# Attention output written as query rows with the values as moving operand, and a mix product from split rows and split output weights

## The reference

```python
h = modulate(rmsnorm(x, g_norm1), sh1, sc1)          # sh1, sc1, gt1, ... from the conditioning vector
p, pc = h @ w_in, hc @ w_in                          # [Fourier 256 | q 768 | k 768 | v 768]
f_out = fourier_mix(p[..., :256], w_fmix)            # (1024, 256)
# 12 heads of 64; a query sees an 8 x 16 window of keys (masked scores) and all 256 context keys, one softmax
na_out = neighbourhood_attention(q, k, v, kc, vc, rpb)   # (1024, 768)
y = concat([rmsnorm(f_out, g_out[:256]), rmsnorm(na_out, g_out[256:])], -1) @ w_out
x = x + gt1 * y
h2 = modulate(rmsnorm(x, g_norm2), sh2, sc2)
x = x + gt2 * hierarchical_moe(h2, ...)              # 32 experts, top 1 group of 4, top 2 of 8 experts
return rmsnorm(x, g_final)
```

## Time and profile before

| | us |
|---|---|
| median of 3 runs | 1379.69 |
| lowest and highest | 1378.57, 1381.49 |
| the profiled execution, its own time | 1377.49 |
| its span, first to last instruction | 1375.2 |
| attention, 371.9 to 571.1 | 199.2 |
| mix, to the end of the last route but one, 571.1 to 709.7 | 138.6 |

### The profile page before, as it was taken

One profiled execution on the slowest core, in us unless ns is written; L12 is line 12 of the kernel. 1 busy time (PEld: TensorE's weight loads), 2 busy tenths in 40 slices (PEclk: granted clock), 3 DMA queues, 4 the chain that ended last, 5 costly groups with the idle time before them and its releaser, 6 DMA issues. The chain is left out here.

```text
span 1375.2 us, 18282 instructions
## 1 busy us (share of the span) xinstructions
PE 1282.1 (93%) x7138; PEld 1020.7 (74%) x7138; DVE 919.9 (67%) x1084; ACT 706.8 (51%) x822; POOL 242.5 (18%) x184
## 2 busy tenths in 40 slices
PE   4799999998899999999976999999999999999965
PEld 1799888887688888645544788888888888888842
DVE  2556543330077877544356988999988988889848
ACT  3742121121266666411113877877778777787713
POOL 0000000001000010100001154254254263521000
PEclk8899999999999999999986999999999999999988
DMA  9548744442486553312124899999999999999755
GB/s 382 198 169 306 248 135 158 157 130 96 169 321 233 190 189 94 130 60 95 61 92 162 347 389 391 389 378 374 389 382 387 384 372 395 383 383 383 255 198 219
DMA packets 96568, 349.73 MB, mean 254 GB/s; under 512 B 14219, under 2 KB 48483, under 8 KB 68835
## 3 DMA queue, kind: packets, MB, share of 16 engines
q1 hardware_dynamic: 79731, 317.35, 61.6%
q10 hardware_dynamic: 7536, 14.42, 3.5%
q0 software_dynamic: 9216, 16.80, 3.2%
HBM read 319.68 MB, written 39.32 MB: 261 GB/s over the span
## 5 line engine op out<-in xcount | busy, mean ns | idle before, releaser
L1825 DVE TENSOR_TENSOR w_low<-raw,w_high 128x2048 fp32r<-128x2048 f32 x128 | 293.4, 2314 | 31.2 <-ACT w_high L1765 28.3
L1765 ACT ACTIVATE w_high<-raw 128x2048 fp32r<-128x2048 f32 x128 | 241.1, 1910 | 9.3 <-PEq L1141 9.3
L1825 DVE TENSOR_TENSOR w_low<-arena,w_high 128x2048 fp32r<-128x2048 f32 x64 | 146.4, 2289 | 30.0 <-ACT w_high L1765 30.0
L1765 ACT ACTIVATE w_high<-arena 128x2048 fp32r<-128x2048 f32 x64 | 122.2, 1909 | 5.2 <-DMA arena<-in_w_down 5.2
L1682 PE MATMUL p_g<-w_high,x_high 128*128 128x512 f32 x256 | 103.9, 406 | 3.2 <-DVE x_low L1830 3.2
L1724 POOL DMA_INDIRECT y_rows<-arena,row x32 | 49.3, 1540 | 325.4 <-ACT arena L1786 323.9
L1682 PE MATMUL p_u<-w_high,x_high 128*128 128x512 f32 x256 | 102.3, 400 | 0.0
L1682 PE MATMUL p_y<-w_high,h_high 128*128 128x512 f32 x256 | 99.7, 389 | 2.5 <-DVE h_low L1835 2.5
L1682 PE MATMUL p_a<-tokens_high,half_high 128*128 128x512 f32 (+1 forms) x272 | 101.8, 374 | 0.0
L1684 PE MATMUL p_g<-w_high,x_low 128*128 128x512 f32 x256 | 101.2, 395 | 0.0
L1683 PE MATMUL p_g<-w_low,x_high 128*128 128x512 f32 x256 | 101.0, 394 | 0.0
(11 more groups left out here) (286 smaller groups left out, 2751.6 us busy)
## 6 DMA issues: line engine op xcount, KB each, us to landing
raw<-in_w_gate SPq DMA_DIRECT2D x64, 1024.0 KB, 8.2
raw<-in_w_up SPq DMA_DIRECT2D x64, 1024.0 KB, 7.6
arena<-in_w_down SPq DMA_DIRECT2D x64, 1024.0 KB, 7.9
raw<-in_w_ada SPq DMA_DIRECT2D x24, 1024.0 KB, 7.0
low_home<-in_bias SPq DMA_DIRECT2D x92, 192.0 KB, 3.8
x<-qk_rows SPq DMA_DIRECT2D x6, 1664.0 KB, 8.0
raw<-in_w_chunks SPq DMA_DIRECT2D x9, 1024.0 KB, 5.4
qk_rows<-x SPq DMA_DIRECT2D x18, 512.0 KB, 2.7
```

Source lines behind the costliest of these rows:

```text
L1765: act.activation(x.high[i % SPLITS][:], x.raw[j][:, :], ACT.Copy).then_inc(high_ok, 1)
L1825: dve.tensor_tensor(x.low[i % SPLITS][:], x.raw[j][:, :], x.high[i % SPLITS][:], ALU.subtract).then_inc(low_ok, 1)
```

## The change

**Attention.** In `weigh` the operands change places: a block of turned probabilities, 128 keys by 128 queries, is stationary, and the 64 channels of the values move. The output tile has the queries on the partitions and is written into `s.x1`, columns hp*128 on. The reciprocal of the row sum is then a number per partition, so the transposed spread copy goes (11 transposes a step become 10, the DVE copy 896 columns become 768, and the copy at line 993 goes), and `normalise` multiplies by it directly. `gain` and the POOL additions go; the last eight steps square the finished row tiles on ACT. Five of the eight blocks of output weights are split into high and low on ACT and DVE in steps 16, 22, 28, 34 and 40. The gain is multiplied into the weights there. The first head pair is loaded into gaps of `s.x1` by four DMAs, the others into the arena.

**Mix.** Token tiles of the attention output and of the Fourier part are transposed (`turn_n`, 8 transposes a tile), split by `high` (ACT) and `low` (DVE), and multiplied with the split weights by `products`. The gate, scale and shift rows are written to DRAM by three DMAs in the attention stage and loaded back as broadcast rows, which replaces `spread`; `turn_f` and the sums over `s.acc` go. The last three blocks of weights are split at the start of this stage.

```diff
-                    for k in range(KEYS // P):
-                        for h in range(2):
+                    for h in range(2):
+                        for k in range(KEYS // P):
...
-                            last = pe.matmul(p_o[n % 2][h * HD:(h + 1) * HD, 0:P], v, probt[b][:, first:first + P],
+                            last = pe.matmul(p_o[n % 2][:, h * HD:(h + 1) * HD], probt[b][:, first:first + P], v,
...
-                    pe.wait_ge(inverted, n + 1)
-                    pe.transpose(p_t[:, 2 * KEYS:2 * KEYS + P], spread[b], s.ident[:]).then_inc(turned, 1)
...
+                    dve.tensor_tensor(rows(s.x1[:, i, hp * P:(hp + 1) * P]), rows(p_o[n % 2][:, 0:P]),
+                                      rinv[:, n % 4, :].unsqueeze(2).to_broadcast([P, 2, HD]), ALU.mult).then_inc(normed, 1)
...
+                for j, x in enumerate((s.gate1, s.scale2, s.shift2)):
+                    sp.dma_start(a.vec_rows[j].rearrange("(k p) -> p k", p=P), x[:], allow_slow_non_contiguous=True).then_inc(s.wo_in, 16)
...
+                    if n == NT:
+                        for k, dst in zip(MIX_ORDER, s.wo_raw):
+                            sp.dma_start(dst, a.w_out[k * P:(k + 1) * P, :].rearrange("p (b n) -> p b n", b=4)).then_inc(s.wo_in, 16)
...
+                def high(n, b):
+                    act.wait_ge(turned, 2 * run_n(n) + b + 1)
+                    if n >= 2:
+                        act.wait_ge(mixed, n - 1)
+                    act.activation(nt_high[n % 2][:, 4 * b:4 * b + 4, :], p_t[b][:].rearrange("p (k q) -> p k q", k=4), ACT.Copy).then_inc(split_high, 1)
...
+                high(0, 0)
                 act.wait_ge(pool_ok, 4)
-                act.wait_ge(sums_ok, 2)
                 act.activation(root[:, 0:2, :], ss[:, 0:2, :], ACT.Sqrt, bias=epsb[:, 0:1]).then_inc(rooted, 1)
...
+                for i in range(EARLY, KD):
+                    split(i)
+                high(0, 1)
...
+                low(0, 0)
                 norm_groups()
...
+                scale_f(0)
+                for i in range(EARLY, KD):
+                    split(i)
+                low(0, 1)
+                for n in range(1, NT):
+                    scale_f(n)
+                low(1, 0)
+                low(1, 1)
+                for n in range(NT):
                     residual(n)
-                    if n < NT - 1:
+                    move_x(n)
+                    if n + 2 < NT:
                         norm_x(n)
-                move_x(NT - 1)
-                norm_x(NT - 1)
+                        low(n + 2, 0)
+                        low(n + 2, 1)
+                    else:
+                        norm_x(n)
...
+                        last = products(pe, p_y[n % 2][:, h, :], nt_high[n % 2][:, i, :], nt_low[n % 2][:, i, :],
+                                        s.wo_high[i][:, w], s.wo_low[i][:, w], start=(i == 0), stop=(i == KD - 1))
...
+                turn_n(0, 0)
                 for n in range(NT):
...
+                    for h in range(2):
+                        mix(n, 0, h)
+                    if n == 0:
+                        turn_n(0, 1)
+                    else:
+                        turn_x(n - 1)
+                    mix(n, 1, 0)
+                    if n + 1 < NT:
+                        turn_n(n + 1, 0)
+                        turn_n(n + 1, 1)
+                    mix(n, 1, 1)
+                    if n == 0:
+                        route_shift()
+                    else:
+                        route(n - 1)
```

More of the change, by code:

```diff
@@ L605, in _ @@
                     act.activation(ft[:, i // 2, (i % 2) * 512:(i % 2 + 1) * 512], p_a[m % 3][:], ACT.Copy).then_inc(moved, 1)
-                act.wait_ge(roped[1], HP)
+                for w in range(2):
+                    act.wait_ge(roped[w], HP)
                 for u in range(AB, G + NT):
@@ L954, in _ @@
                                            accum_out=rsum[n % 2][:, h:h + 1]).then_inc(exped, 1)
-                    if n >= 6 and (n - 2) % 4 == 0:
-                        u = (n - 2) // 4 - 1
-                        gain(u // 2, u % 2)
-                gain(HP - 1, 1)
+                    if n in SPLIT_AT:
+                        split(SPLIT_AT[n])
+                    if n >= STEPS - NT + 3:
+                        square(n - (STEPS - NT + 3))
+                square(NT - 1)
             @block.vector
@@ L1011, in _ @@
                         normalise(n - 2)
+                    if n - 1 in SPLIT_AT:
+                        split(SPLIT_AT[n - 1])
             @block.tensor
@@ L1031, in far @@
                         first = P + LOC + h * L
-                        return pe.matmul(p_s[:, first:first + L], qp[b][rows, q], kc[b][rows, :], start=True, stop=True)
+                        return pe.matmul(p_s[:, first:first + L], h_.q[0][rows, i, :], h_.context[rows, :], start=True, stop=True)
                     far(0).then_inc(scored, 1)
@@ L1265, in norm_groups, with scale_f, low, split @@
                     step(tt(ratio[:], ratio[:], rstd[:, 0, :], ALU.mult))
[L1266 to L1275 removed]
+                def scale_f(n):
+                    ts(s.fout[:, n, :], s.fout[:, n, :], ratio[:, n:n + 1], None, ALU.mult).then_inc(scaled, 1)
+                def low(n, b):
+                    dve.wait_ge(split_high, 2 * n + b + 1)
+                    part = slice(4 * b, 4 * b + 4)
+                    tt(nt_low[n % 2][:, part, :], p_t[b][:].rearrange("p (k q) -> p k q", k=4), nt_high[n % 2][:, part, :], ALU.subtract).then_inc(split_low, 1)
+                def split(i):
+                    k = MIX_ORDER[i]
+                    dve.wait_ge(s.half_high, WO_FIRST + i + 1)
+                    quarters = lambda x: x[:].rearrange("p (b n) -> p b n", b=4)
+                    stt(quarters(s.wo_low[i]), s.wo_raw[i], s.vcol[:, 80 + k:81 + k], quarters(s.wo_high[i]), ALU.mult, ALU.subtract).then_inc(s.half_low, 1)
                 def residual(n):
@@ new lines, in mix @@
+                def mix(n, b, h):
+                    if b == 0 and h == 0 and n >= 2:
+                        pe.wait_ge(added, 2 * (n - 2) + 1)
+                    if h == 0:
+                        pe.wait_ge(split_low, 2 * n + b + 1)
+                    for i in range(4 * b, 4 * b + 4):
+                        if n == 0 and h == 0:
+                            pe.wait_ge(s.half_low, WO_FIRST + i + 1)
+                        w = slice(h * 512, (h + 1) * 512)
+                        last = products(pe, p_y[n % 2][:, h, :], nt_high[n % 2][:, i, :], nt_low[n % 2][:, i, :],
+                                        s.wo_high[i][:, w], s.wo_low[i][:, w], start=(i == 0), stop=(i == KD - 1))
+                    if b == 1 and h == 1:
+                        last.then_inc(mixed, 1)
@@ L1455, in route_shift @@
                     last.then_inc(logits, 1)
+                turn_n(0, 0)
                 for n in range(NT):
-                    last = pe.matmul(p_r[:, n:n + 1], s.acc[:, n * P:(n + 1) * P], s.ones[:, 0:1], start=True, stop=True)
-                last.then_inc(sums_ok, 1)
-                spread(0, s.gate1)
-                pe.wait_ge(s.wo_in, 16)
-                mix_na(0)
-                turn_f(0)
-                mix_na(1)
-                mix_f(0)
-                spread(2, s.scale2)
-                mix_f(1)
-                spread(3, s.shift2)
-                mix_na(2)
-                turn_f(1)
-                mix_f(2)
-                turn_x(0)
-                mix_na(3)
-                route_shift()
-                route(0)
-                turn_x(1)
-                mix_f(3)
-                route(1)
-                turn_x(2)
-                for n in range(4, NT):
-                    mix_na(n)
-                    if n == 4:
-                        route(2)
-                    turn_x(n - 1)
-                    mix_f(n)
-                    route(n - 1)
+                    for h in range(2):
+                        mix(n, 0, h)
+                    if n == 0:
+                        turn_n(0, 1)
+                    else:
+                        turn_x(n - 1)
[4 more added lines that the diff above has]
+                    mix(n, 1, 1)
+                    if n == 0:
+                        route_shift()
+                    else:
+                        route(n - 1)
                 turn_x(NT - 1)
@@ L2185, in build @@
         s.raw = [m.sb(f"raw{r}", [P, CHUNK]) for r in range(RING)]
-        flat = s.x1[:].rearrange("p a b -> p (a b)")
-        s.heads = [flat[:, (1 - b) * 4 * D:(1 - b) * 4 * D + 3 * N + L] for b in range(2)]
         s.vh = s.raw[2][:].rearrange("p (g n) -> p g n", g=16)
```

312 lines of the change are left out of this document (137 added, 175 removed).

## The result

The kernel after the change takes 1405.22 us in the median of four executions (1404.08 to 1406.08), the kernel before 1380.51 (1378.57 to 1381.49). The ratio is 1.018 with a 95% interval of 1.0163 to 1.0198: slower by 24.7 us. The forecast was 1406. The profiled execution of after took 1405.07 us with a span of 1403.2; for before these are 1377.49 and 1375.2.

What follows compares the result with a forecast made beforehand. The prediction took PE to bound attention and mix, the only stages touched. The profiled 1377.5 us + 39.4 for attention - 12.9 for the mix gave 1404.0, or 1406 us on the scale of the runs, with bounds of 1397 to 1421.

Steps and rivals of the forecast that it cites:

- What bounds the kernel: Attention and mix: PE bounds both, busy 193.5 of 199.2 us and 138.2 of 138.6 us.
- The attention step, +39.4: Attention: 20 full-array instructions at 0.108 us in `weigh` make a step 4.79 us against 3.97, +39.4 us in 48 steps.
- DMAs at nothing in attention: Attention: output weight loads, three scattered stores and first head pair's loads cost nothing; 5 us late would show once.
- The mix, -12.9: Mix up to the end of `route(6)`: 12.9 us gained, the 0.9 of the earlier stage start included; bounds -20 and -4.
- The 6.5 us of idle PE: Mix, first tile: PE stands still about 6.5 us, for late group norms and three weight splits ahead of `low(0,1)`.
- the second fall of the clock: Mix, behind the idle stretch of the first tile: PE's clock falls once more, costing 2.5 us.
- The first fall: Mix, first 24 split products: the clock falls to 1.2 GHz, costing 2.1 us.
- the tile: Mix, each steady token tile: split products, two transpose groups and `route` take 14.35 us against 16.39.
- 1 (loads do not count): Attention, `weigh`: second instruction or load does not count at 64 moving columns, 10 us gained there, total 1357; 6%.
- 2 (loads and movement add): Attention, `weigh`: load and movement times add, 20 x 0.053 us more each step, +51 us, total 1457; 4%.
- 3 (the mix gains nothing): Mix: the ACT, DVE, PE chain or late norms take what the products give, total 1419; 10%.
- 4 (the start costs nothing): Mix start: no cost there, for instance if router weights land earlier, total 1399; 8%.

Runs made afterwards that it cites:

- e1: The changed kernel with each value matmul moving 128 columns of values in place of 64; attention stage 241.4 us, 1406.5 us in one run.
- e2: The changed kernel with 64 queries stationary in place of 128, the others left out; attention stage 202.9 us, total time not comparable.
- e8: e5 with the three scattered row stores issued twice in the old place; 1368.6 us, 0.9937 of the kernel before.
- e3: The changed kernel with the norms' root on ACT no longer waiting for the scaled router weights; 1400.7 us, 1.0157 of the kernel before.
- e4: The changed kernel with the old attention (values stationary, heads side by side) and the new mix kept; 1371.2 us, 0.9944 of the kernel before.
- e5: e4 with the norms' root no longer waiting for the scaled router weights, the edit of e3; 1359.2 us, 0.9858 of the kernel before.
- e7: e5 with the three scattered row stores issued behind the attention stage's last load; 1356.9 us, 0.9843 of the kernel before.
- e6: The changed kernel with two broadcast gate row loads issued behind the router weights' load, not ahead; 1402.0 us, 1.0167 of the kernel before.

## Why the prediction was right, step by step

**What bounds the kernel.** PE bounds both stages after the change too, but for the first tile of the mix, and the sum could be made of PE's distances and the one wait there.

**The attention step, +39.4.** Measured 4.81 us for 4.79: `score` 1.38 as said, `turn` 1.15 as said, `weigh` 2.28 for 2.26. An instruction with 128 by 128 loaded and 64 columns moving costs 0.109 us for the 0.108 taken. e1 and e2 show the reason to be the one given. The mix begins 39.5 us later (610.67 for 571.13), where the forecast, less the 0.9 us of the earlier change of stage, had 38.5; 48 steps at 0.02 more are the difference.

**DMAs at nothing in attention.** In the profiled execution of after this held: PE waits nowhere past the first ten microseconds. But it had no margin. The three scattered stores were named and costed at nothing, "if one were late by 5 us it would show once". They hold up the tables behind them, and e8 shows the price when one is needed, 5.59 us. e3, e4 and e5 lost time there to standstills, whose tie to the stores is not shown: in e3 2.79 us, and with the low clock behind it (0.60 from 407.0 to 411.4) a stage 5.7 us longer than after's. From e5 to e7, which moves the stores away, the stage is 2.7 us shorter and the median 2.3.

**The mix, -12.9 (-12.0 from its own start).** Measured -9.5. The mechanism was right: first split product, stall on the norms, DVE's splits ahead of `low(0,1)`, low clock behind it. The 6.5 us of idle PE came as two waits, 2.93 us for the scaled Fourier rows and 3.50 for `nt_low`, 6.43 together, and the second fall of the clock cost 2.5 us, as forecast. The first fall was put at 2.1 us, while the row that it quotes gives 4.30 x (1 - 0.60) = 1.7; after paid 1.8 (24 products in 7.26 us for 24 x 0.228 = 5.47), and the stall hid the difference. Two terms count for the miss. First the start: the product behind the stall came 17.25 us into the stage, where 586.6 - 570.2 = 16.4 was forecast. The sentence "the router weights come in no earlier now" missed that they come later: 9.87 us into the stage for 7.77 before (and for the 8.7 that the forecast's root at 579.60 implies, with its stage beginning at 570.2), because two broadcast loads had been put ahead of them. e6 puts the price of that order at 3.6 us of the stage; had the forecast followed the queue instruction by instruction, as it did on PE, it would have been seen. Second the tile: 14.53 us for 14.35, 1.2 us over seven tiles. The stretch between the two, from that product to the end of `route_shift`, took another 0.3 us more than forecast. e3 gives the price of the whole wait for the router weights, 8.3 us of the stage, of which the time gave back about half; in e5 the same edit brought 9.0 of the stage and 11.9 of the time (0.9858 for 0.9944), so how much of it lasts to the end is not settled by these runs.

**What is left to chance.** The rest of the program was forecast as unchanged and was 2.0 us shorter in this profile. The table shows 664.5 to 668.3 us for the same code, so this is the scatter of one execution. The forecast of 1404.0 for the profiled execution, 1405.1 measured, was thus nearer than its terms: 1.2 us too little for attention (39.7 for 38.5) and 2.4 for the mix, against 2.0 from the rest and 0.6 from the start and from what lies outside the span. The errors cancelled; that the forecast is within 1.1 us is partly luck. The lower end of its range stands twice in the prediction, as 1397 in the sum and as 1394 in the chances; the sum gives 1397.

**The rivals.** 1 (loads do not count) and 2 (loads and movement add) fall with e1 and e2. 3 (the mix gains nothing) falls with after's own profile, 9.5 us gained, although the late norms that it named are real. e4, whose mix turns only the Fourier blocks, gains 13.2 us in the stage and 0.56%, 7.7 us, in the time. 4 (the start costs nothing) describes e3, not the change.

## What to carry to other kernels

Before swapping the two operands of a product, count the columns loaded against the columns moved and look whether the old form ran side by side on two halves of the array: here the swap halved what moves, nearly doubled what `weigh` pays (1.25 to 2.28 us), and made the attention stage of a 1380 us kernel 39.7 us longer, while the split product, kept alone in e4, brought 8. When a change adds DMAs, write down the queue in order, and put a load that someone waits for ahead of those that nobody does. A store of single numbers is cheap in bytes and dear in packets: issue it where the DMA engines are idle and no load waits behind it.

## What the runs showed of the hardware beyond the forecast

- Full-array float32 instructions with a load each: 20 take 2.28 us with 64 columns moving and 2.32 with 128, the change of shape included; with 64 columns loaded and 64 moving they take 1.31. So at these sizes the load hides the movement, but half a load is not half the price.
- 3072 packets of four bytes, 12 KB in all, held back some 2 MB of loads (0.81 MB in the window in e5, 2.94 in e7). Issued twice, they made DVE wait 6.90 us for a table. The same stores at 545 us, with DMA 0.15 busy in 540 to 570, held nobody.
- A wait of PE can cost more than its own length: in after, the twelve products behind the waits of 2.93 and 3.50 us ran 0.43 us apart for 0.228, at a granted clock of 0.50 (the lower level, 1.2 GHz), 2.5 us on top of the waits. In e6, with one wait of 3.75 us, they ran 0.43 apart too. In e3, with 1.41 us of waiting at the same place, the granted clock stayed at 1.00.
- The same load of the router weights lands 4.3 us after its issue with two broadcast rows behind it on the queue (e6), and 7.0 us with them ahead of it (after).
